# Two weight chunks per rounding and per subtraction, and six chunks ahead instead of seven, in an encoder layer in fp32r

## What is computed

```python
f1 = swiglu_ffn(rms_norm(h, g1), ffn1_w_in, ffn1_w_out)     # (silu(x W_g) * (x W_u)) W_out, D_FF = 5632
h = h + 0.5 * rms_norm(f1, g1_post)
mix = hybrid_mixer(rms_norm(h, g2), w_in, b_gate, sink_a, rpb_b, w_up_a, w_up_b, w_out)
h = h + rms_norm(mix, g2_post)
f2 = swiglu_ffn(rms_norm(h, g3), ffn2_w_in, ffn2_w_out)
h = h + 0.5 * rms_norm(f2, g3_post)
```

## Time and profile before

| | |
|---|---|
| median of 3 runs | 2113.44 us (2110.95 to 2114.13) |
| the profiled execution | 2111.76 us, its span 2110.0 us |
| TensorE matmuls | busy 2070.3 us, 98% |
| VectorE | busy 1190.8 us, 56%, of it `WL` 997.6 us (1456 of 691 ns) |
| ScalarE | busy 1099.3 us, 52%, of it `WH` 909.9 us (1456 of 631 ns) |
| GpSimd | busy 48.5 us, 2% |
| DMA | 398.75 MB, 189 GB/s |
| granted TensorE clock | 0.994 of full speed on average |

### The profile page before, as it was taken

How to read it: one execution, slowest core, us unless ns; L and a number is a source line. 1 busy time by engine, 2 the same in 40 slices (tenths; PEclk the granted TensorE clock), 3 DMA queues, 4 the chain that set the end, 5 groups by cost and what they waited for, 6 DMA issues and landing times.

```text
span 2110.0 us, 27249 instructions
## 1 busy us (share of the span) xinstructions
PE 2070.3 (98%) x9285; PEld 1711.1 (81%) x9285; DVE 1190.8 (56%) x1856; ACT 1099.3 (52%) x1867; POOL 48.5 (2%) x83
## 2 busy tenths in 40 slices
PE   8999999999999989999999999999999999999997
PEld 6888888888778878888888888788888888888886
DVE  5555555555355565555666665665555555555554
ACT  6555555554444454444555554465555555544442
POOL 1000000000000011110000000000000000000000
PEclk9999999999999999999999999999999999999999
DMA  7666666666566657776555556566666666666663
GB/s 239 191 193 193 193 193 189 193 192 195 167 207 194 194 159 223 215 223 178 160 160 160 170 189 210 161 189 184 191 189 190 187 184 194 190 211 191 195 193 131
DMA packets 204763, 398.75 MB, mean 189 GB/s; under 512 B 13784, under 2 KB 13832, under 8 KB 204304
## 3 DMA queue, kind: packets, MB, share of 16 engines
q1 hardware_dynamic: 200352, 385.95, 60.0%
q0 software_dynamic: 4336, 11.82, 2.6%
HBM read 393.78 MB, written 3.92 MB: 188 GB/s over the span
## 4 chain that ended last, share of the span: by engine, by line
PE 93%; issue 3%; DVE 2%; DMA 1%; ACT 0%; POOL 0%; SPq 0%; DVEq 0%; POOLq 0%; ACTq 0%
PE acc L815 30%; PE acc L817 30%; PE acc L816 30%; PE tp L855 1%; PE tp L911 1%; PE tp L934 1%; PE tp L836 1%; PE tp L922 0%; DVE h L603 0%; DMA rpb_padded<-rpad 0%; PE tp L901 0%; DMA raw<-in_ffn_w_in 0%; DVE tmp L642 0%; DMA raw<-in_w_in 0%; DVE WL L529 0%
## 5 line engine op out<-in xcount | busy, mean ns | idle before, releaser
L529 DVE TENSOR_TENSOR WL<-raw,WH 128x512 fp32r<-128x512 f32 x1456 | 997.6, 691 | 859.4 <-ACT WH L340 854.9
L340 ACT ACTIVATE WH<-raw 128x512 fp32r<-128x512 f32 x1456 | 909.9, 631 | 953.7 <-PE acc L817 925.2
L815 PE MATMUL acc<-WH,XH 128*128 128x512 f32 x2080 | 824.4, 396 | 1.9 <-DVE WL L529 1.4
L817 PE MATMUL acc<-WH,XL 128*128 128x512 f32 x2080 | 812.0, 390 | 0.0
L816 PE MATMUL acc<-WL,XH 128*128 128x512 f32 x2080 | 811.4, 390 | 0.0
L817 PEld LDWEIGHTS acc<-WH,XL 128*128 128x128 f32 x2080 | 391.5, 188 | 82.9
L815 PEld LDWEIGHTS acc<-WH,XH 128*128 128x128 f32 x2080 | 392.0, 188 | 81.5 <-issue 3.0
L816 PEld LDWEIGHTS acc<-WL,XH 128*128 128x128 f32 x2080 | 392.3, 189 | 78.6
L815 PE MATMUL acc<-WH,MH 128*128 128x512 f32 x704 | 274.8, 390 | 8.2 <-DVE WL L529 8.2
L816 PE MATMUL acc<-WL,MH 128*128 128x512 f32 x704 | 274.4, 390 | 0.0
L817 PE MATMUL acc<-WH,ML 128*128 128x512 f32 x704 | 274.3, 390 | 0.0
(11 more groups left out here) (87 smaller groups left out, 603.3 us busy)
## 6 DMA issues: line engine op xcount, KB each, us to landing
raw<-in_ffn_w_in SPq DMA_DIRECT2D x352, 512.0 KB, 4.3
raw<-in_ffn_w_out SPq DMA_DIRECT2D x176, 512.0 KB, 4.4
raw<-in_w_in SPq DMA_DIRECT2D x136, 512.0 KB, 3.9
raw<-in_w_out SPq DMA_DIRECT2D x32, 512.0 KB, 4.5
raw<-in_w_up_a SPq DMA_DIRECT2D x16, 512.0 KB, 4.2
raw<-in_w_up_b SPq DMA_DIRECT2D x16, 512.0 KB, 4.5
gates<-in_b_gate POOLq DMA_DIRECT2D x16, 256.0 KB, 6.6
h<-in_x SPq DMA_DIRECT2D x4, 512.0 KB, 7.9
```

The source lines that it names most:

```text
L340: act.activation(WH[:, c % WS, :], raw[:, c // 2 % RAW, c % 2, :], ACT.Copy).then_inc(hi_ready, 1)
L529: dve.tensor_tensor(WL[:, c % WS, :], raw[:, c // 2 % RAW, c % 2, :], WH[:, c % WS, :].bitcast(F32), ALU.subtract).then_inc(lo_ready, 1)
L815: pe.matmul(a, hi[:, tok], WH[:, w, :], start=first, stop=False)
L817: mm = pe.matmul(a, lo[:, tok], WH[:, w, :], start=False, stop=last)
```

## The change

`split_hi` and `split_lo` do nothing for an odd chunk, and for an even one they treat it and the next one in one operation of 1024 elements per partition. The waits change with it: ScalarE waits until chunk c - 7, not c - 8, is done, VectorE for both chunks of `hi_ready`, and TensorE waits for `lo_ready` ahead of even chunks only, for both chunks. `AHEAD` becomes 6.

```diff
-AHEAD = WS - 1
+AHEAD = WS - 2
...
             def split_hi(c, more=0):
 
-                if c % 2 == 0:
-                    act.wait_ge(raw_landed[c // 2 % RAW], 16 * (c // 2 // RAW + 1) + more * (16 // (2 * RAW)))
+                if c % 2:
+                    return
+                act.wait_ge(raw_landed[c // 2 % RAW], 16 * (c // 2 // RAW + 1) + more * (16 // (2 * RAW)))
                 if c >= WS:
-                    act.wait_ge(chunk_done, c - WS + 1 + more)
-                act.activation(WH[:, c % WS, :], raw[:, c // 2 % RAW, c % 2, :], ACT.Copy).then_inc(hi_ready, 1)
+                    act.wait_ge(chunk_done, c - WS + 2 + more)
+                w = c % WS
+                act.activation(WH[:, w:w + 2, :], raw[:, c // 2 % RAW, :, :], ACT.Copy).then_inc(hi_ready, 2)
...
             def split_lo(c, more=0):
 
-                dve.wait_ge(hi_ready, c + 1 + more)
-                dve.tensor_tensor(WL[:, c % WS, :], raw[:, c // 2 % RAW, c % 2, :],
-                                  WH[:, c % WS, :].bitcast(F32), ALU.subtract).then_inc(lo_ready, 1)
+                if c % 2:
+                    return
+                dve.wait_ge(hi_ready, c + 2 + more)
+                w = c % WS
+                dve.tensor_tensor(WL[:, w:w + 2, :], raw[:, c // 2 % RAW, :, :],
+                                  WH[:, w:w + 2, :].bitcast(F32), ALU.subtract).then_inc(lo_ready, 2)
...
             def chunk(c, b, hi, lo, first, last, more=0):
 
-                pe.wait_ge(lo_ready, c + 1 + more)
+                if c % 2 == 0:
+                    pe.wait_ge(lo_ready, c + 2 + more)
```

## The result

The changed kernel takes 2178.47 us in the median of four runs (2176.63 to 2180.04), against 2113.03 us before (2110.95 to 2114.13): a ratio of 1.031, with a 95% interval of 1.030 to 1.032. It is 65.4 us slower; the prediction was 2167 us with a range of 2150 to 2188. The profiled execution took 2176.63 us.

The account below looks back on a forecast made before the run. TensorE, busy for 98% of the span, bounds the kernel. Profiled 2111.8 us plus 45.9 (13.6 + 1.0 + 27.1 + 4.3 - 0.8 + 0.7) plus 8.0 of clock gave 2165.7, forecast as 2167 us for the median, range 2150 to 2188.

Parts of the forecast that it names:

- The first QKV block: First of seven QKV blocks, already waiting for late weights: only the wider operations count, 1.0 us taken, between 0 and 2.27.
- The shift, 2.27 us: Work behind an even chunk comes 2.27 us later: 1.30 for one chunk more to wait for, 0.97 for wider operations.
- The widths themselves: Operations of 1024 elements on ScalarE and VectorE: about 1.07 and 1.23 us, 0.44 and 0.535 more than now.
- halfway from 2130 to 2167 us: Rival of more slack: wider operations cost nearly nothing, some 17 us lost, 2130 us; halfway to the forecast 2145; chance 0.10.
- The clock, 8 us: Seven new idle times of about 2.5 us (six QKV blocks, first gate block): five clock falls at 1.6 us, 8 us.
- The rival with a fall behind the waits of 1.5 us too: Clock falls also after the sixteen waits of 1.4 to 1.6 us: 2196 us, or 2180 for half; chance 0.15.
- The gate blocks, 27.1 us: Eight gate blocks: stalls of 1.37, 0.35 and 1.55 us at c = 7, 9 and 13, 27.1 us in all.
- The up-projection: turn_m at c = 5 in the up-projection and first block behind it: 1.08 us at four sites, 4.3 us.
- The FFNs, 0 with 0.2 us of slack: turn_m at c = 5, 22 times: the gate product still ends 0.2 us before TensorE comes, so no cost.
- FFN loops that stretch: Sign that the forecast is wrong: FFN stretches growing longer would show the 0.2 us of slack were not there.
- The wait for the post gain, -0.8: FFN 1, second output block, TensorE dry for 8.20 us: -1.36 and +0.53 for the wider first operation, -0.8 us.
- The start, 0.7: Kernel start: the first matmul waits for the first pair, 0.97 us later; between 0 and 0.97, 0.7 taken.

Follow-up runs that it names:

- run 2: Kernel before, one chunk per operation, ScalarE waiting for one more chunk done ahead of an even chunk, AHEAD = 6: 2138.01 us, ratio 1.012.
- run 3: Changed kernel with VectorE's subtractions put back to one chunk each, ScalarE still rounding two: 2156.01 us, ratio 1.020.
- run 4: Changed kernel with ScalarE's roundings put back to one chunk each, VectorE still subtracting two: 2161.36 us, ratio 1.023.
- run 5: Changed kernel with only the QKV blocks' read_qkv moved from behind chunk 8 to behind chunk 7: 2150.42 us.
- Run 6: Changed kernel with only the gate blocks' side work moved to stand behind chunks whose pair is not late (read_gate behind 14): 2142.59 us.
- run 7: Changed kernel with side work of QKV and gate blocks, mix_b and the gate product moved off late pairs: 2106.32 us, 0.9966 of the kernel before.
- run 11: Changed kernel with only GpSimd's eight stores of the padded bias put 40 chunks apart instead of 48: 2167.53 us.
- run 12: Kernel before with only GpSimd's eight stores of the padded bias put 40 chunks apart instead of 48: 2102.42 us.

## Why the forecast was right, and where it was off

**The mechanism and the sites.** The mechanism was right: all sites that were named wait; the one that was named and costed at nothing, in the FFNs, is told below. Runs 2 to 7 show the shift and both its parts. The size was short by a fifth: 65 us for 54, at 2178.47 us above the 2158 to 2176 us that had a chance of 0.60, and close to the 2180 us that was given for half of the sixteen shorter waits followed by a fall of the clock. None was; the missing time is in the terms below. The first QKV block grew by 0.8 (forecast 1.0), since the piece of weights was late for both chunks alike.

**The shift, 2.27 us: measured, 2.41.** A QKV block after:

```profile
816.54 1.06 ACT L342 ACTIVATE WH<-raw 128x1024 fp32r<-128x1024 f32 x1 [1.66 <-PE acc L823]
...
818.84 1.40 DVE L647 TENSOR_SCALAR tmp<-acc,rstd 128x512 f32<-128x512 f32 x2
...
820.30 1.97 PE L907 MATMUL tp<-ident,tmp 128*128 128x128 f32 x8 [2.52 <-DVE tmp L647]
```

From the split to the read are 2.30 us (1.27 + 0.97 = 2.24 forecast). And the chunk more to wait for costs TensorE's 1.36 us, as run 2 shows, not the 1.30 that was read between two starts of ScalarE. TensorE's wait is 1.05 us longer than in run 2 (2.52 for 1.47), so the shift is 1.36 + 1.05 = 2.41. The blocks are 27.00 us apart where TensorE's clock falls (874.09 to 901.09 in the chain), 4.00 more than before: 2.4 of shift and 1.6 of clock. Run 6, which has the same QKV blocks, gives the same price: from one `turn_qk` to the next are 25.67 us there without a fall (821.49 to 847.16) and 27.23 in the changed kernel with one (820.30 to 847.53).

The widths themselves came out within 0.01 us, though the forecast took its slopes from rows that are not "at the same types", as it says: on ScalarE the row of 256 elements writes fp32r and that of 512 writes f32, and all four read accumulators or `tp`, not `raw`. That it fitted so well was in part luck. Two sums of the rivals are off too, and nothing hangs on it: halfway from 2130 to 2167 us is 2148, not 2145, and the three terms before it add up to 16 us, not 17.

**The clock, 8 us: the number came out, by luck.** Five falls of seven were forecast for the new idle times of 2.5 us. Five came (six with that of the first block, which the kernel before has too), all in the QKV blocks, at 1.6 us each. The stretches of 4 us behind the seven `turn_qk`:

```profile
793.60:797.60 4.00, 3.99 (x16) 3.58 (x17) 0.00 (x0) 0.12 (x1) 0.00 (x0) 0.66 1.04 279
820.30:824.30 4.00, 4.00 (x15) 3.58 (x16) 0.00 (x0) 0.00 (x0) 0.00 (x0) 0.58 0.40 133
847.50:851.50 4.00, 3.97 (x13) 3.33 (x14) 0.00 (x0) 0.23 (x1) 0.00 (x0) 0.57 0.35 118
874.10:878.10 4.00, 4.00 (x15) 3.41 (x16) 0.00 (x0) 0.03 (x1) 0.00 (x0) 0.59 0.37 128
901.10:905.10 4.00, 4.00 (x16) 3.32 (x17) 0.00 (x0) 0.29 (x1) 0.00 (x0) 0.63 0.39 129
928.10:932.10 4.00, 4.00 (x17) 3.32 (x18) 0.00 (x0) 0.54 (x1) 0.00 (x0) 0.67 0.36 121
955.10:959.10 4.00, 4.00 (x22) 3.45 (x23) 0.25 (x1) 1.06 (x1) 0.00 (x0) 1.00 0.36 127
```

Six at 0.57 to 0.67 of full speed, the last at 1.00. Nothing in the forecast says which of them fall. The first gate block's idle time of 2.7 us was not followed by a fall here, and the same one was in run 5 (the changed kernel, then run 5):

```profile
1009.70:1013.70 4.00, 3.56 (x18) 2.74 (x19) 2.60 (x6) 1.54 (x2) 0.00 (x0) 1.00 0.63 211
```

```profile
983.00:987.00 4.00, 4.00 (x13) 3.28 (x14) 1.93 (x5) 0.79 (x1) 0.00 (x0) 0.59 0.63 210
```

The rival with a fall behind the waits of 1.5 us too is refuted: behind none of the gate blocks' waits of 1.4 and 1.6 us did the clock fall, nor in the QKV blocks of run 2, behind idle times of up to 1.7 us (run 2, 780 to 990 us, the sixth column behind the length is the clock):

```profile
780.00:990.00 210.00, 199.32 (x900) 163.42 (x898) 115.65 (x186) 89.01 (x162) 29.71 (x49) 1.00 0.71 208
```

**The gate blocks, 27.1 us: this term was too small by 5.5.** The rows of one block after:

```profile
1061.84 0.39 PE L823 MATMUL acc<-WH,XL 128*128 128x512 f32 x1
...
1062.34 1.06 ACT L342 ACTIVATE WH<-raw 128x1024 fp32r<-128x1024 f32 x1 [3.40 <-PE acc L823]
...
1064.65 0.68 DVE L693 TENSOR_TENSOR prob_b<-tp,biasB 128x512 f32<-128x512 f32 x1
...
1068.64 0.39 PE L823 MATMUL acc<-WH,XL 128*128 128x512 f32 x1
...
1070.45 0.66 PE L928 MATMUL tp<-ident,prob_b 128*128 128x128 f32 x4 [1.43 <-DVE prob_b L710]
```

The transpose was due at 1068.64 + 0.23 = 1068.87 and started at 1070.45, a stall of 1.58, forecast 1.37. At c = 9 it was 0.60 (0.35), of which the kernel before already has 0.08, and at c = 13 1.78 (1.55). Two steps of the forecast were too short, and one was left out:

- The shift. Counted from the pair's split, the chain to the first transpose took 8.11 us where 7.98 was forecast, and the split itself starts 0.50 us behind the last matmul of chunk 1 (1061.84, 1062.34) where the single split of chunk 9 before started 0.42 behind it (1028.29, 1028.71). That is the 0.2 at c = 7.
- "A transpose follows some 0.05 us after it". It does at c = 7, but at c = 9 and 13 it started 0.14 us behind the end of its input (at 1082.93, behind `YL`, which ended at 1082.79).
- Behind a stall the transposes take longer, since their weight loads are no longer ahead of them: 0.41 us to the next matmul (1070.45 to 1070.86), where before it was 0.35 (1035.32 to 1035.67), and 0.75 for 0.67 at c = 13.

Together 0.7 us a block, and 4.0 instead of 3.3 us for each. The up-projection has the same error, 0.2 us at each of its four sites (1.31 each for 1.08).

**The FFNs, 0 with 0.2 us of slack: the slack was not there.** Before, then after:

```profile
109.26 1.03 PEld L855 LDWEIGHTS tp<-ident,tmp 128*128 128x128 f32 x8
109.49 1.04 PE L855 MATMUL tp<-ident,tmp 128*128 128x128 f32 x8
```

```profile
109.32 1.41 DVE L570 SCALAR_TENSOR_TENSOR tmp<-acc,rstd,tmp 128x512 f32<-128x512 f32 x2
...
110.61 0.39 PE L823 MATMUL acc<-WH,XL 128*128 128x512 f32 x1
110.85 0.85 PEld L861 LDWEIGHTS tp<-ident,tmp 128*128 128x128 f32 x8 [0.28 <-issue]
110.86 1.09 PE L861 MATMUL tp<-ident,tmp 128*128 128x128 f32 x8
```

After, VectorE is done at 109.32 + 1.41 = 110.73, and the transpose was due at 110.61 + 0.23 = 110.84. The slack is 0.11 us, not 0.23, since the shift is 2.41 and not 2.27; and the transpose started 0.13 us behind its input, not 0.05. So the 0.2 us were used up by the two errors of the gate blocks, and the stall is 0.02. The weight load, whose operand is the tile that VectorE writes, ran 0.23 us ahead of the matmul before, under the last chunk; after, it starts with it, and the eight transposes take 0.84 us to the next matmul instead of 0.80. Together 0.07 us a round in FFN 1 (44.50 us on average for 44.43) and 0.19 in FFN 2 (44.62), where VectorE's pair starts 0.12 us later still. That is 2.5 us over the nineteen rounds between the transposes of the chains, and with the hooks moved it is gone (44.43 us a round in run 7). The profile does not show what the load waits for in its last 0.12 us. The forecast's own sign of being wrong, "FFN loops that stretch", came.

**The wait for the post gain, -0.8: the gain came and was taken back.** The idle time fell from 8.20 to 6.74 us, but the clock then stayed at its lower level (1.2 GHz) for 5.8 us of matmuls, 585.82 to about 591.5, and not for 2.9 (583.91 to 586.9). The 2.9 us more at half speed cost half of that, which is the 1.46 saved. The stretch behind the wait, before and then after:

```profile
584.00:587.50 3.50, 3.50 (x10) 2.79 (x11) 3.46 (x6) 0.00 (x0) 0.00 (x0) 0.59 0.66 209
```

```profile
584.00:592.00 8.00, 6.18 (x16) 4.83 (x16) 5.17 (x6) 0.58 (x1) 0.00 (x0) 0.53 0.53 156
```

Runs 11 and 12 agree: with the gain in time the kernel with pairs saves 10.9 us and the one without 10.1, so the pairs had not gained 0.8 here. The step that failed is the term itself: it shortened the wait and left the time at the lower clock behind it as it was.

**The start, 0.7:** 1.3, but one execution can't tell the two apart. Runs 5 and 6 have the same code as the changed kernel up to there, and their first `turn_m` stands at 68.05 and 66.17 us, against its 66.51.

**The quoted rule.** The second half of the rule in the Trainium skill (Perfetto Trace Analysis, Optimizing Scalar/DVE Operations), that breaking up instructions may let work finish sooner where an unsaturated engine causes bubbles on others, holds here only through the place of the side work: run 7 has the joined operations, no bubble of TensorE at its side work, and loses nothing.

The errors are nearly all to one side, 11 us together: slack was read to the hundredth, and each hand-over was costed at its shortest.

## What to carry to other kernels

In a pipeline of slots like this one, joining two steps delays the first of them by a whole period of the consumer (1.36 us here), whatever the operation itself gains: look for everything that is queued behind the *first* half of a pair, and put it behind the second half of the pair before. What stands behind the second half of its own pair is late too, but only by the width (`copy_probT`). Costing that move needs three rows a site: the release, the operation in front of the hook, and the consumer's arrival. Take the consumer's own period for the chunk more, and leave at least 0.15 us between a result and its transpose: 0.05 to 0.14 were measured here, and slack under that is none. Where no such site was left, joining was worth nothing in this kernel, whose joined engines are not the bound: 100 us less of VectorE's time changed the whole by 0.15 us, and not for the better.

## What was not expected of the hardware

- Idle times of TensorE of up to 1.7 us were not followed by a slower clock in run 2. Those of 2.5 us or more were in six cases of eight in the kernel after, at 1.6 us each. In run 3 five QKV blocks have the same idle time of 1.92 us, and the clock fell behind three of them: blocks 26.39 us apart stand beside others 24.81 us apart in the chain, and the longer ones have the fall (0.67 of full speed behind 869.04 and 920.24, 1.00 behind 895.43):

```profile
869.04 1.09 PE tp L903 x8
895.43 1.09 PE tp L903 x8
920.24 1.09 PE tp L903 x8
```

  So between 1.9 and 2.8 us the length of the idle time alone does not decide it, and these runs do not show what else does. The gate blocks' waits of 1.4, 0.4 and 1.6 us within 13 us did not make it fall.
- The wait for the post gain became 1.46 us shorter and saved nothing, since the slow stretch behind it became twice as long. Where a fall of the clock follows, the idle time and the time behind it have to be read together.
- TensorE's chunk pace did not move by a hundredth when half of its semaphore waits were taken out (1.36 us per six matmuls in all kernels).
